# Two-layer block and two mixers on one core: cumulated decays spread through DRAM instead of by TensorE, query-key product made transposed

## The reference, cut to what matters

```python
gcum = jnp.cumsum(g, axis=-1)
decay = jnp.exp(jnp.where(tril, gcum[..., :, None] - gcum[..., None, :], NEG_INF))
a = jnp.where(strict, jnp.einsum('bhnid,bhnjd->bhnij', k_beta, k) * decay, 0.0)
sol = lax.linalg.triangular_solve(eye + a, rhs, left_side=True, lower=True, unit_diagonal=True)
qk = jnp.einsum('bhnid,bhnjd->bhnij', q, k) * decay
...
o_i = jnp.einsum('bhcd,bhde->bhce', q_i, state) + jnp.einsum('bhcj,bhje->bhce', qk_i, v_new)
```

## Time and profile before

| what | value |
|---|---|
| median of three runs | 1898.7 us |
| profiled execution, whole | 1899.05 us |
| its span (first to last instruction) | 1897.2 us |
| PE busy | 1888.0 us |
| PE weight loads busy | 1649.0 us |
| DVE busy | 1460.1 us |
| ACT busy | 1083.3 us |
| GpSimd busy | 82.6 us |
| read from HBM | 327.91 MB |

### The profile page before, as it was taken

One profiled execution on the slowest core, in us unless ns is written; L12 is line 12 of the kernel. 1 busy time (PEld: TensorE's weight loads), 2 busy tenths in 40 slices (PEclk: granted clock), 3 DMA queues, 4 the chain that ended last, 5 costly groups with the idle time before them and its releaser, 6 DMA issues.

```text
span 1897.2 us, 32403 instructions
## 1 busy us (share of the span) xinstructions
PE 1888.0 (100%) x11807; PEld 1649.0 (87%) x11807; DVE 1460.1 (77%) x2316; ACT 1083.3 (57%) x1683; POOL 82.6 (4%) x61
## 2 busy tenths in 40 slices
PE   9999999999999999999999999999999999999999
PEld 9888998788988888899987888889888889888888
DVE  7777896877777777778778777777578888888887
ACT  6555764664555555567647645555346655775654
POOL 0000011010000000000110010000000000110000
PEclk9999999999999999999999999999999999999999
DMA  6656553445455555555434455565755555545654
GB/s 236 199 189 197 171 188 102 134 152 170 155 190 188 187 186 190 188 183 185 155 112 145 145 172 179 186 197 180 207 179 178 198 189 173 162 143 158 200 186 143
DMA packets 116717, 330.87 MB, mean 174 GB/s; under 512 B 10896, under 2 KB 40208, under 8 KB 116496
## 3 DMA queue, kind: packets, MB, share of 16 engines
q1 hardware_dynamic: 114496, 325.64, 53.2%
q10 hardware_dynamic: 2128, 3.94, 0.6%
HBM read 327.91 MB, written 1.64 MB: 174 GB/s over the span
## 4 chain that ended last, share of the span: by engine, by line
PE 93%; DVE 4%; ACT 2%; DMA 1%; issue 0%; POOL 0%; ACTq 0%
PE ps L2318 89%; DVE w_lo L1319 1%; DMA raw<-stream 1%; PE ps L2344 1%; ACT w_hi L616 1%; PE ps L2617 1%; PE ps L2871 0%; DVE arena L2133 0%; DVE sc L1831 0%; PE ps L3035 0%; PE ps L2812 0%; PE ps L2893 0%; ACT gates L1113 0%; PE ps L2688 0%; DVE tmp L2176 0%
## 5 line engine op out<-in xcount | busy, mean ns | idle before, releaser
L1319 DVE TENSOR_TENSOR w_lo<-raw,w_hi 128x1024 fp32r<-128x1024 f32 x614 | 750.2, 1229 | 223.6 <-ACT w_hi L616 222.5
L2318 PE MATMUL ps<-w_hi,a_both 128*128 128x512 f32 (+2 forms) x2368 | 753.1, 387 | 1.1 <-DVE a_both L2105 0.7
L616 ACT ACTIVATE w_hi<-raw 128x1024 fp32r<-128x1024 f32 x614 | 637.2, 1053 | 160.8 <-DMA raw<-stream 106.0
L2318 PE MATMUL ps<-a_both,w_hi 128*128 128x256 f32 (+1 forms) x3360 | 712.4, 341 | 0.1
L2318 PEld LDWEIGHTS ps<-a_both,w_hi 128*128 128x128 f32 x3360 | 580.7, 190 | 72.8 <-issue 0.8
L2318 PEld LDWEIGHTS ps<-w_hi,a_both 128*128 128x128 f32 x2368 | 441.9, 188 | 88.6 <-issue 1.2
L2318 PE MATMUL ps<-w_lo,a_both 128*128 128x512 f32 (+2 forms) x1184 | 455.4, 385 | 0.0
L2318 PE MATMUL ps<-a_both,w_lo 128*128 128x256 f32 x2592 | 448.1, 283 | 0.0
L2318 PEld LDWEIGHTS ps<-a_both,w_lo 128*128 128x128 f32 x2592 | 380.5, 191 | 8.9
L2318 PEld LDWEIGHTS ps<-w_lo,a_both 128*128 128x128 f32 x1184 | 223.2, 188 | 36.5
L689 ACT ACTIVATE a_both<-arena 128x256 fp32r<-128x256 f32 x132 | 55.2, 419 | 139.4 <-DVE arena L1433 98.7
(11 more groups left out here) (349 smaller groups left out, 1186.7 us busy)
## 6 DMA issues: line engine op xcount, KB each, us to landing
raw<-stream SPq DMA_DIRECT2D x613, 512.0 KB, 3.5
arena<-upad SPq DMA_DIRECT2D x8, 284.0 KB, 6.0
gates<-late ACTq DMA_DIRECT2D x1, 1088.0 KB, 8.7
out<-tmp SPq DMA_DIRECT2D x3, 256.0 KB, 2.3
upad<-arena ACTq DMA_DIRECT2D x2, 288.0 KB, 8.1
con<-consts SPq DMA_DIRECT2D x1, 560.0 KB, 5.1
raw<-stream ACTq DMA_DIRECT2D x1, 512.0 KB, 3.8
x<-x_in ACTq DMA_DIRECT2D x2, 256.0 KB, 5.1
```

Source lines behind the costliest of these rows:

```text
L616: nc.scalar.activation(laid(w_hi, u), loaded(u), ACT.Copy).then_inc(hi_ready, 1)
L1319: V.tensor_tensor(laid(w_lo, u), loaded(u), laid(w_hi, u), ALU.subtract).then_inc(split_ready, 1)
L2318: return nc.tensor.matmul(o, a, b, start=start, stop=stop, **k)
```

## The change

Cumulated decays. A new operation of SP stores `sc[:, 72:80]` into DRAM transposed, as 1024 single elements of 4 bytes (`store_cum`, queued behind the load of unit moba 1, waiting for "cumcp"), and another reads the resulting 4 KB row back into all 128 partitions, 512 KB (`spread_cum`, queued behind the load of moba 4, waiting for the store). DVE builds E from this tile `rows` instead of from banks 6 and 7. PE's 8 products "R" are gone.

Query-key product. PE swaps the operands, so the product comes out with keys as rows. It needs a transposed decay, ET: DVE adds a transposed mask to `rows` (2 new operations behind the keys `kgd`), ACT takes 8 more exponentials with the negated cumulated value as bias (one more small DVE operation makes it), and DVE multiplies the product with ET straight into QKT. PE's 8 transposes and ACT's copy are gone. `rows` lies in arena columns 11264 to 12288, where O comes later, ET where QK was.

```diff
+        ET = gup[:, 2048:3072].rearrange("p (a b) -> p a b", b=128)
+        rows = reg(11264, 8, PART)
+        cumd = [nc.dram_tensor(f"cumd{l}", (8, PART), F32, kind="Internal").ap() for l in range(DEPTH)]
 # sync queue
+            def store_cum(l):
+                sp.wait_ge(*DV.at(l, "cumcp"))
+                sp.dma_start(cumd[l].rearrange("b p -> p b"), sc[:, 72:80], allow_slow_non_contiguous=True).then_inc(cum_stored, 16)
+            def spread_cum(l):
+                sp.wait_ge(cum_stored, 16 * (l + 1))
+                sp.dma_start(flat(rows), cumd[l].rearrange("b p -> (b p)").unsqueeze(0).broadcast_to([PART, 8 * PART])
+                             ).then_inc(cum_spread, 16)
...
+                        if u == POS["moba", l] + 1:
+                            store_cum(l)
+                        if u == POS["moba", l] + 4:
+                            spread_cum(l)
 # ScalarE
                 split(POS["z", l] + AHEAD)
+                act.wait_ge(*DV.at(l, "ET"))
+                for b in range(8):
+                    e = nc.scalar.activation(ET[:, b, :], ET[:, b, :], ACT.Exp, bias=sc[:, 280 + b:281 + b])
+                e.then_inc(*AC.sig(l, "ET"))
                 turned_copy(0)
-                act.wait_ge(*PE.at(l, "QKT"))
-                nc.scalar.activation(QKT, ps[:, 4:6, :], ACT.Copy).then_inc(*AC.sig(l, "QKT"))
...
+                        act.wait_ge(*DV.at(l, "QK"))
                         nc.scalar.activation(sB, flat(mqkv[:, 2:4, :]), ACT.Square).then_inc(*AC.sig(l, "mobasq"))
 # VectorE
                         tick(V.tensor_copy(gqk, ps[0:LD, 6, 128:129]))
+                        tick(V.tensor_scalar(sc[:, 280:288], bank(6, 0, 8), -1.0, None, ALU.mult))
                         V.tensor_copy(sc[:, 72:84], bank(6, 0, 12)).then_inc(*DV.sig(l, "cumcp"))
...
-                dve.wait_ge(*PE.at(l, "R"))
+                dve.wait_ge(cum_spread, 16 * (l + 1))
                 for t in range(2):
-                    i = V.scalar_tensor_tensor(E[:, 4 * t:4 * t + 4, :], bank(6 + t).rearrange("p (a b) -> p a b", b=128), -1.0,
+                    i = V.scalar_tensor_tensor(E[:, 4 * t:4 * t + 4, :], rows[:, 4 * t:4 * t + 4, :], -1.0,
                                                each(const("causal"), 4), ALU.mult, ALU.add)
...
                                 ).then_inc(*DV.sig(l, "kgd"))
+                for t in range(2):
+                    i = V.tensor_tensor(ET[:, 4 * t:4 * t + 4, :], rows[:, 4 * t:4 * t + 4, :],
+                                        each(const("causalt"), 4), ALU.add)
...
+                i.then_inc(*DV.sig(l, "ET"))
...
+                dve.wait_ge(*AC.at(l, "ET"))
                 dve.wait_ge(*PE.at(l, "QK"))
                 for t in range(2):
-                    i = V.tensor_tensor(QK[:, 4 * t:4 * t + 4, :], bank(4 + t).rearrange("p (a b) -> p a b", b=128),
-                                        E[:, 4 * t:4 * t + 4, :], ALU.mult)
+                    i = V.tensor_tensor(QKT[:, 4 * t:4 * t + 4, :], bank(4 + t).rearrange("p (a b) -> p a b", b=128),
+                                        ET[:, 4 * t:4 * t + 4, :], ALU.mult)
 # TensorE
-                ev(DV, "c_lo")
-                for b in range(8):
-                    i = mm(bank(6 + b // 4, 128 * (b % 4), 128 * (b % 4) + 128), sc[:, 240 + b:241 + b].broadcast_to([PART, 128]), const("tri"))
-                i.then_inc(*PE.sig(l, "R"))
                 ev(AC, "gsq")
...
-                ev(DV, "Et")
+                ev(DV, "c_lo")
                 blocks(6, lambda o, tt, h: nc.tensor.transpose(o, kT(tt, h), ident), "ktok")
                 pe.wait_ge(m_ready, 3 * l + 3)
-                blocks(4, lambda o, tt, h: mm(o, qT(tt, h), kT(tt, h)), "QK")
+                blocks(4, lambda o, tt, h: mm(o, kT(tt, h), qT(tt, h)), "QK")
                 ev(DV, "kgd")
                 z_unit(0)
                 z_unit(1)
                 pair_turn(0)
-                ev(DV, "QK")
-                blocks(4, lambda o, tt, h: nc.tensor.transpose(o, QK[:, 4 * tt + h, :], ident), "QKT")
                 ev(DV, "vb")
```

More of the change, by code:

```diff
@@ L198 @@
     [("ident", 128), ("tri", 128), ("id64", 64), ("m0", 64), ("m0t", 64), ("mt", (LEVELS - 2) * 64), ("causal", 128),
-     ("cosm", TT * 32), ("sinm", TT * 32), ("cosl", TT * 16), ("sinl", TT * 16), ("rows", TAP_ROWS)])
+     ("cosm", TT * 32), ("sinm", TT * 32), ("cosl", TT * 16), ("sinl", TT * 16), ("rows", TAP_ROWS), ("causalt", 128)])
 LATE, N_LATE = columns([("dneg", 9 * 128), ("wa", 512), ("wx", 512)])
@@ L229, in constants @@
         neg += [same, band, same]
+    put("causalt", np.where(causal.T, 0.0, NEG).astype(np.float32))
     put("causal", np.where(causal, 0.0, NEG).astype(np.float32))
@@ L267 @@
 BASE = LEVELS - 2
-LV_STEPS = ([("T", 0), "QKT"] + [s for m in range(1, BASE) for s in (("U", m), ("X", m), ("T", m))]
+LV_STEPS = ([("T", 0)] + [s for m in range(1, BASE) for s in (("U", m), ("X", m), ("T", m))]
             + [("U", BASE), ("X", BASE), ("T", BASE), ("U", BASE + 1), ("T", BASE + 1)])
-PE_STEPS = (["cums", "cT", "R", "G", "stat", "AT", "vtok", "ktok", "QK"] + LV_STEPS
+PE_STEPS = (["cums", "cT", "G", "stat", "AT", "vtok", "ktok", "QK"] + LV_STEPS
             + ["u", "wT", "S1", "ob0", "wS", "oa", "mobakT", "ob1", "mobaT", "oT", "qT0", "qT1", "kT0", "kT1"])
-DVE_STEPS = (["z0", "cvar", "g", "cumcp", "gld", "silu", "c_lo", "Et", "gvar", "A", "X0", "kgd", "vb", "XT0", "QK", ("X", 1), ("X", 2), "mobavar"]
+DVE_STEPS = (["z0", "cvar", "g", "cumcp", "gld", "silu", "c_lo", "Et", "gvar", "A", "X0", "kgd", "ET", "vb", "XT0", "QK", ("X", 1), ("X", 2), "mobavar"]
              + [("X", m) for m in range(3, BASE)] + [("V", BASE), ("T", BASE + 1), "mobaqk"]
@@ L275 @@
                 "mlavark", "qrope", "mlak", "mlavarq"])
-ACT_STEPS = (["sm", "spe", "csq", "cn", "egc", "kds", "c_hi", "gsq", "E", "AT", ("T", 0), "QKT", ("U", 1), "mobasq"]
+ACT_STEPS = (["sm", "spe", "csq", "cn", "egc", "kds", "c_hi", "gsq", "E", "AT", "ET", ("T", 0), ("U", 1), "mobasq"]
              + [s for m in range(2, BASE) for s in (("T", m - 1), ("U", m))]
@@ L354, in build @@
         ev_scaled = sem("ev_scaled")
+        cum_stored, cum_spread = sem("cum_stored"), sem("cum_spread")
         cf_th, sc_copy, pair_read, b_read = sem("cf_th"), sem("sc_copy"), sem("pair_read"), sem("b_read")
@@ L588, in _ @@
                             spread_u(p)
+                    for l in range(DEPTH):
+                        if u == POS["moba", l] + 1:
+                            store_cum(l)
+                        if u == POS["moba", l] + 4:
+                            spread_cum(l)
             for b in range(2):
@@ L1807, in mixer @@
                                 ).then_inc(*DV.sig(l, "kgd"))
+                for t in range(2):
+                    i = V.tensor_tensor(ET[:, 4 * t:4 * t + 4, :], rows[:, 4 * t:4 * t + 4, :],
+                                        each(const("causalt"), 4), ALU.add)
+                    if t == 0:
+                        tick(i)
+                i.then_inc(*DV.sig(l, "ET"))
                 dve.wait_ge(*PO.at(l, "grs"))
@@ L2774, in mixer @@
                 back(m, (0,))
-                ev(AC, "QKT")
+                ev(DV, "QK")
                 for q, f, e in corners:
```

## The result

The changed kernel takes 1914.6 us (median of four runs, 1911.4 to 1918.4) beside 1898.4 us of the kernel before: ratio 1.0087, 95% interval 1.0074 to 1.0100. It is 16 us slower; 1893.5 us was forecast, and 1899.0 us was the end of the range. The profiled execution is one of the shorter ones, 1911.9 us with a span of 1910.1 us, 12.9 us over that of before.

A forecast was written before the change was run, and what follows sets the result against it. PE was taken to bound the kernel, busy 1888.0 of 1897.2 us. 2 x (1.79 + 0.87) = 5.32 us off PE, less 0.15 at kgd, gave 5.2 us: 1898.7 to 1893.5 us, range 1892.8 to 1899.0.

The forecast's parts named there:

- the price of the store: Store behind load moba 1: 64 pieces per DMA engine, taken at 10 to 20 ns each.
- The delay d of the load of moba 2: Load issued 1.3 us behind the store: no delay expected; a layer gains 2.66 - 0.1 - d.
- the sum's own rule: DVE ahead of kgd: delays count in full after the change; before, there was about 1.7 us of room.
- The bound from above: Store's price from the earlier large store: 190 ns a row, halved to 100 ns, so 64 pieces take 6.4 us.
- Rival (c): Third rival: store blocks the queue at 100 ns a piece, load moba 2 5.1 us late; 5.1 us lost, 1903.8 us; chance 0.16.
- The estimate of 0.3 us: Store of 4 KB, from the skill's strided DMA transpose being 19 times slower than the crossbar one: 0.3 us.
- R's 1.79 us: PE ahead of group G: removing the 8 products R frees 1.79 us and 16 entries a layer.
- the forecast 0.87 us a layer: PE ahead of the solve: removing the 8 QK transposes frees 0.87 us a layer.
- the next gate: DVE's kgd ahead of z 0: PE stopped 0.1 to 0.15 us in layer 0, about nothing in layer 1.
- The additions of ET: DVE behind kgd: two additions, 1.2 to 1.3 us; DVE then waits some 0.4 us for ACT; covered.
- The latency of both transfers: Store and broadcast before DVE wants `rows`: covered, 15 us for a broadcast whose median landing is 3.5 us.
- (a): Store felt at 50 ns a piece, load moba 2 1.9 us late: 1.1 us gain, 1897.6 us; chance 0.19.

The follow-up runs named there:

- e5: Kernel before plus only the transposed store and SP's wait for it, its 1024 elements landing 64 B apart; 1898.3 us, ratio 1.0004.
- e7: Kernel before plus only the transposed store and SP's wait, with 512 pieces of 4 B, 4 B apart; 1913.3 us, ratio 1.0081.
- e3: Changed kernel with the store issued from ACT's queue and the broadcast moved behind the load of moba 6; 1914.1 us, ratio 1.0080.
- e12: Kernel before plus only the transposed store and SP's wait, its 1024 elements landing 8 B apart; 1904.7 us, ratio 1.003.
- e4: Kernel before plus only a store of the same 4 KB, not transposed, as 128 touching pieces of 32 B, and SP's wait; 1897.8 us, ratio 0.9999.
- e6: Kernel before plus only the transposed store and SP's wait, its 1024 elements landing 512 B apart; 1898.0 us, ratio 1.0002.
- e10: Kernel before plus only the transposed store and SP's wait, its 1024 elements landing 32 B apart; 1898.0 us, ratio 1.0001.
- e8: Changed kernel with decays made in rows by an added PE product, stored as 8 rows of 512 B, broadcast behind moba 7; 1894.0 us, ratio 0.9983.
- e11: e8 with the query-key part of the kernel before (additions, transposes and copy), so only R is gone; 1894.2 us, ratio 0.9982.
- e9: Kernel before plus only a broadcast of a 4 KB weight row into 128 partitions behind the load of moba 4; 1898.05 us, ratio 1.0002.
- e1: Kernel before plus only the store of 1024 touching 4-byte elements and SP's wait for it at moba 4; 1915.4 us, ratio 1.0090.
- e2: Changed kernel with decays made in rows by an added PE product, stored as 8 rows of 512 B, broadcast behind moba 4; 1894.5 us, ratio 0.9981.

## Why the prediction was wrong

**The step that failed** is the price of the store: "I take 10 to 20 ns, near the lower end, as bytes make up most of the 34 ns row", and from it that "up to 1.3 us of store (20 ns a piece) delays nothing". The delay d of the load of moba 2 was put at 0; it is 8.0 us. The price of passing an engine can be read from e5, timeline of ACT, where the touching is taken away:

```profile
249.65 1.06 ACT L628 ACTIVATE w_hi<-raw 128x1024 fp32r<-128x1024 f32 x1 [3.37 <-DMA raw<-stream]
```

The load is 0.7 us late there. With the 1.3 us of lead that the store has, 64 pieces took 2.0 us, 31 ns each by the sum's own model: more than my 20, and absorbed, as the run loses nothing. (The kernel before has 1.7 us of room at kgd; in the changed kernel, by the sum's own rule, a d of 0.7 would have taken 1.4 us off the gain.) What was missing is a term that no row of before could show and that I didn't leave room for: what happens to 1024 writes to touching addresses after the engines have passed them. Dividing the store by pieces was the wrong model, whichever row gave the price; e7 shows it, where half the pieces land no sooner. The bound from above was misread as well. The large store of the earlier trace rows is 288 KB, which is 256 rows of 1152 B and not 512: 16 rows an engine, 381 ns each, 190 after the halving, and 12.2 us for 64 pieces. That bound would have held the 10.2 us, though for a wrong reason.

**Rival (c)** had the right place: the store holds what is behind it, load moba 2 is late, DVE stands. Its price by the piece was of the wrong kind, and not only the store's own queue is held (e3). Its size fell short, d = 5.1 us and 5.1 us lost against 8.0 and 16. Its account, 2 x (d + 0.1 - 2.66), gives 10.9 us with the true d; the solve of layer 1 starts 15.1 us late, and 5.1 of that are the lower clock that PE gets after standing, a term that the sum did not have. The median of the runs holds more of that term: the mean granted clock was 0.997 and 0.996 in the two runs of 1911.9 and 1911.4 us, 0.992 and 0.993 in those of 1917.2 and 1918.4. Its path differed as well: PE was stopped at the splits and at the squares ahead of G, not at kgd. And by e12 a loss comes earlier than I wrote ("It turns into a loss from d = 2.56 us on"): there d = 1.8 us has grown to 3.3 us at a later split and costs 5.9 us in both layers with R still there, where the sum's own rule, with 1.7 us of room at kgd, gives 0.2. With R gone that room is gone too; that kernel with d = 1.8 was not run.

**The rules weighed** pull apart in the same way. The Trainium skill, "DMA: Bandwidth & Descriptors" (Specifications), has transfers below 512 B read, modify and write; it made the third rival likelier. But every piece here is below 512 B, and e4, e5, e6 and e10 cost nothing: small size alone isn't the price in this case. The estimate of 0.3 us worked out from the Trainium skill, "VectorE: DVE Perf Modes" (The three transpose paths), is off from the 10.2 us to landing by a factor of about 30.

**What came right.** R's 1.79 us and 16 entries a layer, and the QK transposes, left PE's list as counted; e8 against e11 gives the forecast 0.87 us a layer for the transposes on PE, of which 1.0 us in all has arrived at the solve of layer 1. kgd is the next gate: e8 is stopped there 0.5 us, in layer 1, where 0.15 was forecast, for layer 0. The additions of ET took longer, a pair 2.51 us against "1.2 to 1.3 us", and were still covered: DVE waited 0.47 us for the exponentials (forecast 0.4), and PE nowhere in the solve. The broadcast was covered in the kernel before (e9). The latency of both transfers was too: E didn't wait for `rows` even with the store landing after 10 us. With the store mended, e8 wins 3.2 us by its ratio, where 5.3 less 0.8 for the added product and 0.5 at kgd is 4.0 us, inside the interval of 1.5 to 4.9 us.

**The signs named ahead** did their work: "The prediction is wrong if [...] the store's landing takes more than 6.6 us, since the broadcast then stops SP ahead of moba 5". It took 10.2 us (9.5 in layer 0), and SP stood 6.6 us in all at the broadcast, in layer 0 until 253.25. Moba 5 was issued at 259.27 instead of 251.33, but not for that: the last 6 us SP waited for DVE's split of the late moba 2, and in e1, without a broadcast, the same load goes at 259.66. ACT's wait beyond 4 us for moba 2, the sign of (a) or (c), is the 10.55 us above.

## What to carry to other kernels

Before a few KB go to memory and back, ask how the pieces lie there, not only how many and how large they are: single elements that touch, written from different partitions, kept the next load 8 us late here, and the same elements 32 bytes apart, or in 128 pieces of 32 bytes, cost nothing. Where a transfer has no like in the trace of before, give its price a bound from the side of the stall of everything behind it, and put the waits that follow in the sum with what they grow to. And count a stop of PE as more than its length, since the clock can fall after it, by 1.7 us of work or by several times that.

## What the runs showed of the hardware

- 1024 writes of 4 bytes to touching addresses in memory land after 10.2 us, 512 of them after 10.0; 8 bytes apart 5.2 us; 32 to 512 bytes apart 3.0 to 3.3 us; 128 pieces of 32 bytes 1.7 us. Until the touching ones land, the loads nearly stand (41 packets in 7 us).
- The store in ACT's queue held the loads of the sync queue as long as in their own (ACT waited 11.22 against 10.55 us).
- After PE had stood 3.0 us, its granted clock was 0.50 for the next 3 us; 16 entries that take 1.95 us took 3.37. In e3 the same stop was followed by 13 us at 0.50. After shorter stops it is mixed: the clock fell after the ones of 2.27 and 2.28 us in e1 (at 292.33 and 929.79) and of 2.48 us in e12, and not after 2.28 us in e1 (at 269.12), 2.22 us in e12 and 2.47 us in e2.
- VectorE reading two operands from SBUF was slower beside GpSimd. Two additions of 128x512 (L1833) took 2.51 us with GpSimd at work from 288.77 to 291.77, the second alone 1.79; 114 additions of that size from SBUF take 0.68 us each (L1448). In layer 1 of e2, where GpSimd had ended before them, the pair took 1.28 us. Two splits took 3.45 us beside GpSimd and 2.35 otherwise, while the kgd operations, which read PSUM, took 0.69 us beside it. GpSimd's own pair took 3.00 to 3.93 us instead of 2.56. No run changes this alone.
